# The branch stage of a hybrid scan and mixture-of-experts layer: its first weights loaded during the scan, the scan's last stores awaited later, weights in thirds, the last stores issued by ScalarE, and the first w_o product taken block by block

## The reference

```
u = h @ w_in                          # h: modulated layer norm of x
z, xbc, dt, b, c, x', gates = split(u)
y = ssd_chunked(...) + xs * d_skip    # a scan over chunks of the sequence
y = rms_norm(y * silu(z), ssd_norm_w) # over 2048 channels
u_a = y @ w_ssd_out                   # 2048 -> 1024
u_b = (b * conv(c * x')) @ w_short_out # 1024 -> 1024
mix = (sigmoid(g_a) * u_a + sigmoid(g_b) * u_b) @ w_o
x = layer_norm(2 ** 0.25 * x + g1 * mix, ln1_g, ln1_b)
```

## Time and profile before

| | us |
|---|---|
| median of 3 runs | 6014.72 |
| lowest and highest | 6014.28, 6020.15 |
| the profiled execution's own time | 6021.4 |
| its span, first to last instruction | 6019.5 |
| mean granted TensorE clock | 0.978 of full speed |

### The profile page before, as it was taken

One profiled execution on the slowest core, in us unless ns is written; L12 is line 12 of the kernel. 1 busy time (PEld: TensorE's weight loads), 2 busy tenths in 40 slices (PEclk: granted clock), 3 DMA queues, 4 the chain that ended last, 5 costly groups with the idle time before them and its releaser, 6 DMA issues. The chain is left out here.

```text
span 6019.5 us, 78484 instructions
## 1 busy us (share of the span) xinstructions
PE 5787.8 (96%) x27606; PEld 4702.5 (78%) x27606; DVE 4259.2 (71%) x3413; ACT 3093.5 (51%) x2841; POOL 912.3 (15%) x698
## 2 busy tenths in 40 slices
PE   6999999998999989999969999999999999999996
PEld 2888888886777768887848888888888888888884
DVE  4333200224566565555879999999999999999996
ACT  5222111003444444442147777777777777777772
POOL 1000000002333320000001111111111111111113
PEclk7999999999999999999979999999999999999998
DMA  6311221113444445555348543316468459532355
GB/s 234 133 70 69 84 73 66 42 52 109 131 139 130 141 158 185 184 183 179 127 161 338 185 150 118 122 31 233 151 217 308 135 208 407 215 93 56 123 212 191
DMA packets 298555, 924.57 MB, mean 154 GB/s; under 512 B 25808, under 2 KB 163280, under 8 KB 260368
## 3 DMA queue, kind: packets, MB, share of 16 engines
q1 hardware_dynamic: 207696, 701.59, 31.6%
q0 software_dynamic: 40800, 170.84, 10.0%
q10 hardware_dynamic: 49920, 50.34, 2.4%
HBM read 744.27 MB, written 178.54 MB: 153 GB/s over the span
## 5 line engine op out<-in xcount | busy, mean ns | idle before, releaser
L2084 DVE TENSOR_TENSOR moe_w_lo<-keep_w_gu,moe_w_hi 128x2048 fp32r<-128x2048 f32 x648 | 1440.8, 2286 | 3.8 <-ACT moe_w_hi L2030 3.8
L2030 ACT CAST moe_w_hi<-keep_w_gu 128x2048 fp32r<-128x2048 f32 x648 | 1239.0, 1913 | 378.7 <-PE moe_ps_gu L1973 192.1
L2090 DVE TENSOR_TENSOR moe_w_lo<-moe_w_dn,moe_w_hi 128x2048 fp32r<-128x2048 f32 x324 | 734.0, 2287 | 31.8 <-ACT moe_w_hi L2040 31.8
L2040 ACT CAST moe_w_hi<-moe_w_dn 128x2048 fp32r<-128x2048 f32 x324 | 620.3, 1915 | 256.2 <-PE moe_ps_gu L1973 256.2
L1973 PE MATMUL moe_ps_gu<-moe_w_hi,moe_hT_hi 128*128 128x512 f32 x2592 | 703.4, 394 | 12.3 <-DVE moe_w_lo L2084 12.3
L166 PE MATMUL prj_ps_p<-h_hi,prj_w_hi 128*128 128x512 f32 x1792 | 699.5, 390 | 7.9 <-DVE prj_w_lo L607 7.9
L166 PE MATMUL prj_ps_p<-h_lo,prj_w_hi 128*128 128x512 f32 x1792 | 699.2, 390 | 0.0
L166 PE MATMUL prj_ps_p<-h_hi,prj_w_lo 128*128 128x512 f32 x1792 | 699.1, 390 | 0.0
L1973 PE MATMUL moe_ps_gu<-moe_w_lo,moe_hT_hi 128*128 128x512 f32 x2592 | 695.0, 390 | 0.0
L1973 PE MATMUL moe_ps_gu<-moe_w_hi,moe_hT_lo 128*128 128x512 f32 x2592 | 694.9, 390 | 0.0
L1973 PEld LDWEIGHTS moe_ps_gu<-moe_w_lo,moe_hT_hi 128*128 128x128 f32 x2592 | 488.1, 188 | 101.5
(11 more groups left out here) (321 smaller groups left out, 9373.2 us busy)
## 6 DMA issues: line engine op xcount, KB each, us to landing
keep_w_gu<-in_w_gu_t SPq DMA_DIRECT2D x128, 2048.0 KB, 9.1
moe_w_dn<-in_w_down_t SPq DMA_DIRECT2D x64, 2048.0 KB, 9.8
rows_scratch<-prj_out POOLq DMA_DIRECT2D x48, 1024.0 KB, 4.4
brn_w<-in_w_branch_t SPq DMA_DIRECT2D x64, 768.0 KB, 6.6
h_w_in<-in_w_in_t SPq DMA_DIRECT2D x80, 512.0 KB, 4.3
moe_b_gu<-b_gu_scratch SPq DMA_DIRECT2D x32, 1024.0 KB
mod_w<-in_w_ada SPq DMA_DIRECT2D x24, 1024.0 KB, 7.4
rows_scratch<-ssd_out ACTq DMA_DIRECT2D x96, 256.0 KB, 2.8
```

Source lines behind the costliest of these rows:

```text
L2030: act.copy(w_hi[n % NB][:], raw(w_gu, n)).then_inc(gu_hi, 1)
L2040: act.copy(w_hi[(GU + n) % NB][:], raw(w_dn, n)).then_inc(dn_hi, 1)
L2084: dve.tensor_tensor(w_lo[n % NB][:], raw(w_gu, n), w_hi[n % NB][:].bitcast(F32), ALU.subtract).then_inc(gu_lo, 1)
L2090: dve.tensor_tensor(w_lo[b][:], raw(w_dn, n), w_hi[b][:].bitcast(F32), ALU.subtract).then_inc(dn_lo, 1)
```

## The change

1. Three tiles of 128 x 1024 for the first branch weights live on through the border. One is the tile that the `w_in` weights were loaded into; the other two lie where the high and low tile 0 of `w_in` weights were. When SyncE has issued all loads of the scan, it waits for the last tile but one to be done and the last split to be made, and loads unit 0's branch weights into them.
2. The ring `out`, the scan's result tiles `yo` and the semaphores of their stores live on too. ScalarE no longer waits for the stores at the end of the scan. In the branch block SyncE waits for the y stores ahead of the first gates, and for the stores of `out` ahead of unit 1's gates; ScalarE waits for one of them ahead of the root. The gates and `rstd` now lie in these tiles.
3. The branch weights are loaded, cast and split in three thirds of 128 x 1024 rather than in two halves of 128 x 1536.
4. The last two results of the branch block are stored by ScalarE, with a semaphore of their own. The output product waits for it where it waits for the other stores, ahead of its tile 12.
5. In the first output tile each block of `w_o` is used for both column halves, before the next block is waited for.
6. POOL clears the semaphores of the branches and the output product at the start of routing instead of at the end of the program.

The diff, without its unchanged lines (and indented less):

```diff
@@ -586,8 +586,7 @@
-    w_hi = [sb(f"w_hi{i}", [P, KD, P], F32R) for i in range(2)]
-    w_lo = [sb(f"w_lo{i}", [P, KD, P], F32R) for i in range(2)]
+    w_hi, w_lo = ([S.w0[i], sb(f"w_{name}1", [P, KD, P], F32R)] for i, name in enumerate(("hi", "lo")))
@@ -820,7 +819,7 @@
-    out = ring("out", NOUT, [P, BANK])
+    out = [S.late[:, i, :] for i in range(NOUT)]
@@ -832,7 +831,7 @@
-    yo = ring("y", 2, [P, GT, P])
+    yo = [S.yo[:, i, :].rearrange("p (a t) -> p a t", a=GT) for i in range(2)]
@@ -842,7 +841,7 @@
-    v_in, bank_out, y_out = sems("ssd_v_in", NOUT), sems("ssd_bank_out", NOUT), sems("ssd_y_out", 2)
+    v_in, bank_out, y_out = sems("ssd_v_in", NOUT), S.bank_out, S.y_out
@@ -941,6 +940,12 @@
+        sp.wait_ge(done, N_WHOLE + N_LATE - 1)
+        sp.wait_ge(w_split, N_WHOLE + N_LATE)
+        apart(sp, S)
+        for c, part in enumerate(S.brn_w):
+          sp.dma_start(part[:], A["w_branch_t"][0:P, c * KD * P:(c + 1) * KD * P].rearrange("p (k m) -> p k m", k=KD)
+                ).then_inc(S.brn_w_in[c], 16)
@@ -1084,10 +1089,6 @@
-        for b in range(NOUT):
-          act.wait_ge(bank_out[b], 16 * BANKS // NOUT)
-        for s in range(2):
-          act.wait_ge(y_out[s], 16 * UNITS // 2)
@@ -1200,19 +1201,19 @@
-    rstd = sb("rstd", [P, BANK])
-    HALF = ITEMS // 2
-    w = [sb(f"w{c}", [P, HALF, P]) for c in range(2)]
+    rstd = S.late[:, 2, :]
+    W3 = ITEMS // KD
+    w = S.brn_w
...
-    gates = [sb(f"gates{i}", [P, 2, BANK]) for i in range(2)]
+    gates = [S.yo, S.late[:, 0:2, :]]
...
-    raw_in, w_in, gates_in = sems("brn_raw", NRAW), sems("brn_w", 2), sems("brn_gates", 2)
+    raw_in, w_in, gates_in = sems("brn_raw", NRAW), S.brn_w_in, sems("brn_gates", 2)
@@ -1238,11 +1239,11 @@
-          for c in range(2):
-            wait(sp, w_split, 2 * u - 1 + c)
+          for c in range(W3):
+            wait(sp, w_split, W3 * u - (W3 - 1) + c)
...
-            sp.dma_start(w[c][:], A["w_branch_t"][bass.ds(n * P, P), c * HALF * P:(c + 1) * HALF * P]
-                  .rearrange("p (k m) -> p k m", k=HALF)).then_inc(w_in[c], 16)
+            sp.dma_start(w[c][:], A["w_branch_t"][bass.ds(n * P, P), c * KD * P:(c + 1) * KD * P]
+                  .rearrange("p (k m) -> p k m", k=KD)).then_inc(w_in[c], 16)
@@ -1265,15 +1266,20 @@
-        load_w(0, 0, 0, 0)
...
+          if tb == 0:
+            for s in range(2):
+              sp.wait_ge(S.y_out[s], 16 * S.y_stores)
...
+          if tb == 0:
+            for b in range(3):
+              sp.wait_ge(S.bank_out[b], 16 * S.bank_stores)
@@ -1305,16 +1311,17 @@
-          store(tb * NU + NU - 2, NU - 2, 0, tb)
-          store(tb * NU + NU - 1, NU - 1, 1, tb)
+          if tb + 1 < TB:
+            store(tb * NU + NU - 2, NU - 2, 0, tb)
+            store(tb * NU + NU - 1, NU - 1, 1, tb)
...
-          for c in range(2):
+          for c in range(W3):
...
-            act.copy(w_hi[s][:, c * HALF:(c + 1) * HALF, :], w[c][:]).then_inc(w_rounded, 1)
+            act.copy(w_hi[s][:, c * KD:(c + 1) * KD, :], w[c][:]).then_inc(w_rounded, 1)
@@ -1340,26 +1347,33 @@
+          if tb == 0:
+            act.wait_ge(S.bank_out[2], 16 * S.bank_stores)
...
-          act.activation(rstd[:], psQ[:], ACT.Sqrt, bias=S.eps[:], scale=1.0 / INNER).then_inc(root_done, 1)
+          act.activation(rstd, psQ[:], ACT.Sqrt, bias=S.eps[:], scale=1.0 / INNER).then_inc(root_done, 1)
...
+        for s in range(2):
+          u, n = TB * NU - 2 + s, NU - 2 + s
+          act.wait_ge(combined, u + 1)
+          apart(act, S)
+          act.dma_start(S.mixin_d[n * P:(n + 1) * P, (TB - 1) * BANK:TB * BANK], ta[s][:]).then_inc(S.last_out, 16)
...
-          for c in range(2):
-            part = slice(c * HALF, (c + 1) * HALF)
-            dve.wait_ge(w_rounded, 2 * u + c + 1)
+          for c in range(W3):
+            part = slice(c * KD, (c + 1) * KD)
+            dve.wait_ge(w_rounded, W3 * u + c + 1)
...
-          dve.tensor_tensor(ta[s][:], psA[s][:], rstd[:], ALU.mult).then_inc(part_a, 1)
+          dve.tensor_tensor(ta[s][:], psA[s][:], rstd, ALU.mult).then_inc(part_a, 1)
@@ -1412,8 +1426,8 @@
-            if k % HALF == 0:
-              pe.wait_ge(w_split, 2 * u + k // HALF + 1)
+            if k % KD == 0:
+              pe.wait_ge(w_split, W3 * u + k // KD + 1)
@@ -1508,8 +1522,10 @@
-              sp.wait_ge(part, 16 * D // P * SEQ // BANK // 2)
+              sp.wait_ge(part, 16 * (D // P * SEQ // BANK // 2 - 1))
...
+            sp.wait_ge(S.last_out, 32)
+            apart(sp, S)
@@ -1565,19 +1581,27 @@
+        def mix_step(t, half, k):
+          s, cols = t % 2, slice(half * BANK, (half + 1) * BANK)
+          for n, (x, w) in enumerate(((mt_hi, wo_hi), (mt_hi, wo_lo), (mt_lo, wo_hi))):
+            last = pe.matmul(psM[s][:, cols], x[s][:, k, :], w[:, k, cols], start=(k == 0 and n == 0),
+                    stop=(k == KD - 1 and n == 2))
+          if k == KD - 1:
+            last.then_inc(mixed, 1)
...
+        def first_mix():
+          pe.wait_ge(m_split, 1)
+          for k in range(KD):
+            pe.wait_ge(wo_split, k + 1)
+            for half in range(2):
+              mix_step(0, half, k)
...
-          s = t % 2
...
-          cols = slice(half * BANK, (half + 1) * BANK)
...
-            if t == 0 and half == 0:
-              pe.wait_ge(wo_split, k + 1)
-            for n, (x, w) in enumerate(((mt_hi, wo_hi), (mt_hi, wo_lo), (mt_lo, wo_hi))):
-              last = pe.matmul(psM[s][:, cols], x[s][:, k, :], w[:, k, cols], start=(k == 0 and n == 0),
-                      stop=(k == KD - 1 and n == 2))
-          last.then_inc(mixed, 1)
+            mix_step(t, half, k)
@@ -1597,7 +1621,8 @@
-        for t in range(TT + 2):
+        first_mix()
+        for t in range(1, TT + 2):
@@ -1736,6 +1761,7 @@
+    nc.clear_and_free_semaphores(S.spent)
@@ -2375,6 +2401,14 @@
+    S.bank_stores, S.y_stores = N_LATE * SEQ // BANK // 3, GROUPS * TT // 2
+    S.y_out, S.bank_out, S.brn_w_in = ([nc.alloc_semaphore(name=f"{name}{i}") for i in range(n)]
+                     for name, n in (("y_out", 2), ("bank_out", 3), ("brn_w", 3)))
+    across = top.enter_context(ExitStack())
...
+    def kept(name, shape):
+      return across.enter_context(nc.sbuf_tensor(f"across_{name}", shape, F32, side="right"))
+    S.prj_w = kept("w0", [P, KD, P])
@@ -2387,7 +2421,7 @@
-        S.prj_w, S.prj_in = sb("w_in", [P, KD, P]), sem("prj_w")
+        S.prj_in = sem("prj_w")
@@ -2396,6 +2430,11 @@
+        S.brn_w, S.w0 = [S.prj_w], []
+        for name in ("hi", "lo"):
+          S.brn_w.append(kept(f"w_{name}", [P, KD, P]))
+          S.w0.append(nc.alloc_sbuf_tensor_at(f"prj_w_{name}0", [P, KD, P], F32R, offset=nc.sbuf_top))
+        S.yo, S.late = kept("y", [P, 2, BANK]), kept("late", [P, 3, BANK])
@@ -2412,9 +2451,14 @@
+      S.last_out = sem("brn_last_stored")
...
+      in_use.extend(S.y_out + S.bank_out + S.brn_w_in)
...
+      across.close()
...
+    S.spent = in_use[:]
+    in_use.clear()
```

More of the change, by code:

```diff
@@ L1399, in _ @@
                     dve.wait_ge(root_done, tb + 1)
-                    dve.reciprocal(rstd[:], rstd[:]).then_inc(rstd_ready, 1)
+                    dve.reciprocal(rstd, rstd).then_inc(rstd_ready, 1)
                     dve.wait_ge(rstd_ready, tb + 1)
```

## The result

The changed kernel takes 6025.82 us (median of 22 runs, 6021.20 to 6029.06), the kernel before on the same chip 6018.70 (22 runs, 6009.77 to 6026.21). The ratio is 1.0012, 95% interval 1.0006 to 1.0017. The forecast was 13.9 us less than before; it came out some 7 us more. In the two profiled executions the spans are 6019.5 and 6021.6 us.

The account below looks back on a forecast made before the run. TensorE, busy 96%, was taken as the bound, with gains only at two stage borders and the first output product: 5.7 + 3.9 + 4.6 - 0.3 = 13.9 us off 6014.7 gives 6000.8, range 5997.5 to 6007.0 (8 in 10).

Parts of the forecast that it names:

- Border one: From scan to branch: earlier SyncE release and early weights bring the first low part 5.9 us sooner, 5.7 us counted.
- rival C: From scan to branch: early weights are waited for all the same, only 1.9 of 5.7 us remains; 6004.6 us, chance 3%.
- The thirds: Branch loop: one more issue, cast and split per unit, hidden except at three token-block borders, 0.3 us lost (0 to 1.5).
- Rival D: Branch unit loop: weights in thirds become its bound, 32 units cost 16 us; 6016.8 us, chance 4%.
- Border two: From branch to output product: ScalarE's last store avoids waiting on POOL's drain, gain 3.9 us (0.6 to 4.2).
- no drain of 4 us on POOL: Sign expected at the border from branch to output product: POOL's 3.99 us drain after the last store is gone.
- First output product: First of 16 output tiles: each w_o block serves both halves, so it ends at 2793.2 against 2797.8, gain 4.6 us.
- the part that was expected to be late next: First output tile: VectorE's residual waits for parameters, sh2 last at about 2795.2; VectorE gains only 2.6 us at once.
- Rival B: First output tile: late parameters cut its gain by 2.1 us, leaving 11.8 in all; 6002.9 us, chance 10%.
- The cleared semaphores: Start of routing: POOL's clearing, at most 1.1 us, is hidden ahead of its constants; nothing counted.
- The sum: Whole kernel: 5.7 + 3.9 + 4.6 - 0.3 = 13.9 us less, 6000.8 us; chance 71%.

Follow-up runs that it names:

- the version with the late parts only: Kernel before with the branch's last two stores by ScalarE and the first w_o product block by block, no tile moved: 6008.87 us against 6019.48, ratio 0.9984.

## Why the prediction was wrong, step by step

**The step that failed.** "The two long stages ahead of and behind this change (the projections and scan, the experts) are not edited in what they compute. So the change can only be worth what TensorE loses at two stage borders and in the first product behind the second one, unless it harms a loop". The first sentence is true, and the second doesn't follow. The diff moves two tiles that the projection and the scan compute with, and the sum had no term for that: it put these stages at nothing, and they took 17.1 and 5.0 us more. The loop that might be harmed was priced for the branch alone. The description of the change says that two raw tiles lie where tile 0 of the `w_in` weights was; it is the other way about, tile 0 was moved to them. The 4% of the span in which the earlier trace rows has TensorE idle made the borders look like the only place, but a 96% busy share says nothing on how fast the busy part goes; 70 matmuls fewer in 1100 us leave it as it was.

The Trainium skill, "TensorE: Matmul & The Clock Gate", section "Step-by-step: what each phase is for", says that TensorE has two independent read ports, and that loading the next tile's weights takes no read bandwidth from the running matmul. By that the move costs nothing. The runs measure a cost: the same instructions start every 226.6 or 233.2 ns by the distance of the two operands. The Trainium skill, "SBUF — State Buffer", section "Operand start alignment", gives the starts that are legal, and says of its own runs that they timed nothing.

**Border one, forecast 5.9 us less to the first low part, 5.7 in all.** Right as far as TensorE's first matmul; the 0.2 us behind it can't be told apart. Rows of the changed kernel's timeline:

```profile
2225.97 0.38 ACTq L1053 DMA_DIRECT2D y_scratch<-across_y  x1
2227.86 0.33 SPq L1239 DMA_DIRECT2D brn_norm_w<-in_ssd_norm_wT  x1
...
2229.44 1.04 ACT L1324 CAST brn_w_hi<-across_w 128x1024 fp32r<-128x1024 f32 x1 [18.41 <-DMA brn_norm_w<-in_ssd_norm_wT]
...
2234.01 1.41 DVE L1398 SCALAR_TENSOR_TENSOR brn_lo<-mix_wo,brn_norm_w,brn_hi 128x512 fp32r<-128x512 f32 x2
```

From the end of the last store's issue, 2226.35, SyncE's first load comes 1.51 us later, against 3.54 before (2210.14 less 2206.60, rows 2): 2.0 us less, forecast 1.9. The first cast stands 1.58 us behind norm_w's issue (forecast 1.6) and waits for it and not for the weights, so rival C is out. The low part comes 7.66 us behind that issue's end, against 13.68: 6.0 less, and TensorE's idle time falls from 16.52 to 10.50.

**The thirds, forecast 0.3 us lost.** No loss to be seen. From the first branch matmul to the last one's end (the next stage's first matmul less its idle time) it is 547.4 us before and 544.0 after. But it is 546.4 in the changed kernel with 224 bytes of padding, whose branch is the same, and 544.1 in the version with the late parts only, which has halves. These 3 us go with TensorE's clock early in the branch (us, PE busy, clock, DMA share, GB/s), first before, then after:

```profile
2221.00:2250.00 29.00, 23.60 (x72) 0.85 0.73 254
```

```profile
2235.00:2262.00 27.00, 21.89 (x72) 0.93 0.82 286
```

As many matmuls, 72, are there in 29 us at a clock of 0.85 and in 27 us at 0.93. Over nine traces, with the clock taken in the 29 us from 0.1 us behind the first matmul's start: at 0.85 or 0.86 the branch takes 546.6 to 547.4 us with halves (three traces) and 546.3 to 547.1 with thirds (three); at 0.90 or 0.94 it takes 544.1 and 545.2 with halves and 544.0 with thirds. Why the clock differs, no run shows. So of the branch's 7.4 us in the table 4.0 are the border's, and the other 3.4 are not to be credited to the change. Rival D, thirds as the bound of the loop, would have been 16 us; it is out.

**Border two, forecast 3.9.** Right, 4.0 (idle 11.24 to 7.27). Rows of after, the last sum, the store and the next block's first cast:

```profile
2781.00 0.69 DVE L1382 TENSOR_TENSOR mix_out<-mix_out,brn_tb 128x512 f32<-128x512 f32 x1
2781.79 0.34 ACTq L1362 DMA_DIRECT2D mixin_scratch<-mix_out  x1
...
2782.57 1.04 ACT L1553 CAST mix_m_hi<-mix_m 128x1024 fp32r<-128x1024 f32 x1 [26.78 <-PEq L1236]
```

The cast follows the store by 0.8 us. By the figures for the first byte in the Trainium skill, "DMA: Bandwidth & Descriptors", section "Specifications", the move would have been worth 0.4 us; the border gained ten times that. One sign was put wrongly, "no drain of 4 us on POOL": the drain is still there and even longer, but it begins 32 us before the block's end, out of the path:

```profile
L1236 POOLq DRAIN  x1: 7756/7756/7756, 2749.8 to 2749.8; - x1
```

**First output product, forecast 4.6.** 4.05 in the changed kernel, 4.5 with the late parts alone: right within its ends. From its first matmul to its 48th's end the first product took 17.8 us before and 13.9 after, where 13.3 was forecast, and TensorE stands still in it no more, against 2.25 and 0.36 us before. VectorE's first residual shows the part that was expected to be late next:

```profile
L1650 DVE TENSOR_TENSOR mix_r<-mix_ps_m,mix_g x17: 684/1224/1225, 2802.2 to 3002.9; 128x1024 f32<-128x1024 f32 x15, 128x512 f32<-128x512 f32 x2
...
  DMA mix_sh<-ada_scratch: 3.6, 1
```

It waits 3.6 us for sh2, and starts 16.1 us behind the first matmul where it was 18.0 before (the earlier trace rows less). VectorE so gains only 1.9 us and the stage still 4, since TensorE sets its pace. Rival B, which left 2.5 us of gain, is out.

**The cleared semaphores, forecast nothing.** Routing is 62.3 us after and 62.7 before.

**The sum.** In the changed kernel with 224 bytes of padding, which differs from the change only in the place of its tiles, border one gives 5.9 (idle 16.52 to 10.61), border two 4.0 (11.24 to 7.28) and the output product 4.1: together 14.0 us, forecast 13.9, and its median is 15.8 below the kernel before, with an interval of 10 to 24. So the three gains of the sum were there, and the forecast would have held but for the term it didn't have. In the change as it stands 17.1 + 5.0 = 22.1 us of slower matmuls stand against 14: 8 us lost by this sum, and 7.1 by the medians.

**The chances.** 71% went to a sum over three places, and the only case on the other side had its price in the branch loop. None of the rivals asked whether a stage that the diff's text leaves alone could run at another rate.

## What to carry to other kernels

Read in a diff not only what is issued, but where each tile comes to lie, for every stage that uses it: the stationary and the moving tile of a matmul like these should start a multiple of 256 bytes of a partition apart, which a small pad gives; for the 512-column fp32r products here that is worth up to 3% of the rate. When a stage grows with no new wait and a full clock, count its matmuls in a fixed stretch, since the busy share stays the same. And test the parts of a change one at a time: two of these were worth 10.6 us alone by the medians (8.5 in the trace), and all of them together were a loss.

## What the runs showed of the hardware that was not expected

- The distance of TensorE's two operands in the on-chip memory, modulo 256 bytes, sets the rate of back-to-back 128x128 by 512 fp32r matmuls with a new stationary tile each: 226.6 ns at 0, 233.2 at 32, 64 and 224, 232.3 at 128, 228.8 at 192 (a mean of 225.8, 229.2 and 231.7, by the pair of tiles). Where either tile starts by itself doesn't decide it. Their own durations in the trace hardly tell (a mean of 390 ns before, 393 after). Why it is so, and why 192 is milder, no run here shows; the weights are loaded while TensorE multiplies (in the stretch of 1100 us of the kernel before for 911.51 us, beside 1100.00 us of matmuls), and a collision of the two reads would fit, but was only argued.
- GpSimd's drain at a block's end, right behind its own last store, takes 3.99 us. Where another engine issues the block's last two stores and GpSimd's drain begins 32 us before the block's end, it takes 7.5 to 7.8 us and costs nothing. Why it is longer there, no run shows. ScalarE's, behind a store of the same size, took 0.15 us.
- The branch differed by up to 3.4 us between traces, with either form of the weights' loads, and the share of full clock granted in its first 29 us went with it. What came ahead of the projection differed as much (146.3 to 150.1 us to its first matmul in the five traces of the table). Differences of two spans below that are not an edit's until a stage's row shows them.
